# All expert-down units as paired products, with 14 low parts per layer made by an accumulating transfer

## The chip, the cores and the metric

The kernel runs on one core of one Trainium2 chip. The metric is device time in microseconds (us) of that core for one call, and less is better. The engines are TensorE (PE; its weight loads are PEld), VectorE (DVE), ScalarE (ACT), GpSimd (POOL) and SyncE (SP).

## What is computed

A two-layer encoder over 256 tokens of width 1024, all float32. Layer 0 mixes tokens by windowed attention, layer 1 by a gated MLP; after each comes a PEER block, in which every token picks experts among 16384 by product keys:

```python
q = (x @ w_query).reshape(T, PEER_HEADS, 2, D_HALF)
s = jnp.einsum('thcd,hckd->thck', q, sub_keys)
s1, i1 = lax.top_k(s[:, :, 0], PEER_TOPK); s2, i2 = lax.top_k(s[:, :, 1], PEER_TOPK)
...
top_s, pos = lax.top_k(cand, PEER_TOPK)          # 16 of 256 pairs of keys, per token and head
gate = jax.nn.softmax(top_s, axis=-1)
a = jax.nn.gelu(jnp.einsum('cd,chkd->chk', xc, expert_down[ic]))
y = jnp.einsum('chk,chkd->cd', a * gc, expert_up[ic])
```

There are 8 heads with 16 experts each. The kernel gathers no expert weights: it multiplies all 16384 experts with all tokens and lets the gates select.

## The kernel before

**Units.** Weights come in units of 128 x 1024 float32 (512 KB). One layer has its mixer's units, 16 query units, 128 down units (unit n holds experts 128 n to 128 n + 127 of `peer_down`) and 128 up units. Four units are a group; the down phase has groups 0 to 31.

**Two parts per operand.** A float32 product is made of products of rounded parts. For each unit SP loads the raw weights into one of four buffers `raw` (`load`, line 335, or `stream`); ACT rounds them into `w_hi` (`split_hi`, L519) two units ahead; DVE subtracts, `w_lo = raw - w_hi`, in two halves (`split_lo_halves`, L839, and `split_lo_half`, L847). `w_hi` and `w_lo` have four buffers each. The activations stand as `x_both`, high and low part side by side.

**A down unit on PE** has one of two forms. `transposed` (L1491 to L1493) runs 24 matmuls of 256 columns: `w_hi x_hi`, `w_lo x_hi`, `w_hi x_lo` for each of eight slices, and needs `w_lo` at once. `pairs` (L1517, L1521) runs eight matmuls of 512 columns, `w_hi` against high and low part together, then eight of 256 columns, `w_lo x_hi`, and needs `w_lo` only for these. A paired product leaves two sums in one PSUM bank: ACT copies one out (`evict`, L742) and DVE adds the other (`sum_of`, L1314). Which down units are paired is written in the table `PAIRED`: groups 0 to 6 and 21 to 31 wholly, groups 7 to 13 the units 0 and 2 of each four, groups 14 to 20 none. That is 86 of 128.

**DVE beside it.** During the query phase and the first 101 down units DVE also searches the best keys of 16 items (2 token tiles x 8 heads), about one item every seven units; the order of its pieces between the low parts is written out by hand.

**POOL beside it** scatters the gates into a table in HBM (`scatter`, L453): 16 items of 16 indirect transfers with 128 elements each, 256 a layer. Their pace is written in `PACE_FROM`: before each pair of them POOL waits for one more unit to be `used` by PE. Pair p, counted from 0, waits until down unit p - 6 is finished. The transfers of one tile also wait for those of its last head (`added`). The first up units need the finished table: SP loads its pieces into `g_t` (L383 for the first token tile, L386 for the second) once all of that tile's transfers have landed, and DVE multiplies with them (L1411 and L1422).

**Semaphores.** `landed` counts raw loads, `hi_done` and `lo_done` the two parts in order of units, `used` the units that PE has finished. SP waits with a load for the `lo_done` of the unit that had the buffer before.

Of the kernel before, what the change touches and what calls it, by code (L numbers as in the profile page):

```python
# [81 lines left out]

PAIRED = ((0, 7, 4), (7, 14, 2), (14, 21, 0), (21, 32, 4))


def paired(n):

    for first, stop, of_four in PAIRED:
        if first <= n // GROUP < stop:
            return n % GROUP in {0: (), 2: (0, 2), 4: (0, 1, 2, 3)}[of_four]  # L90


# [34 lines left out]
def build(nc, x, attn_units, sg_units, query_units, down_units, up_units, sub_keys, rel_table, bucket_map, sink,  # L127
# [5 lines left out]
    with ExitStack() as ctx:  # L133
# [96 lines left out]

        gain_row = part(HI + 10240, D)

        psum = ctx.enter_context(nc.psum_tensor("psum", [P, 8, 512], F32))
# [13 lines left out]
        hi_done = sem("hi_done")  # L247
        lo_done = sem("lo_done")
        used = sem("used")
        p1_read = sem("p1_read")  # L250
# [78 lines left out]
        l0 = [dict(mix=0, up=MIX_OPERANDS), dict(mix=MIX_OPERANDS + NK, up=MIX_OPERANDS + NK + FT)]  # L329

        block = ctx.enter_context(nc.Block())


        @block.sync
        def _(sp):
            def load(n, source, i=0):

                if not (isinstance(i, int) and n < RAW):
                    sp.wait_ge(lo_done, i * GROUP + (n - RAW + 1))
                sp.dma_start(raw[n % RAW][:, :], source).then_inc(landed[n % RAW], 16)  # L340
# [18 lines left out]
            for layer in range(DEPTH):  # L359
# [8 lines left out]
                stream(u["query"], QUERY_UNITS, queries, 1)  # L368
                stream(u["down"], NK, rows(down_units[layer]))

# [28 lines left out]
        def _(pool):  # L399
# [40 lines left out]
            def scatter(layer):  # L440

                pool.wait_ge(zeroed, 16 * (layer + 1) * (NK // ZERO_UNITS))
                flat = bass.AP(gates[layer].tensor, 0, [[1, NK * P * T], [1, 1]])
                for m in range(ITEMS):
                    t, head = m % TT, m // TT
                    pool.wait_ge(gate_done, ITEMS * layer + m + 1)
                    pool.wait_ge(named, ITEMS * layer + m + 1)
                    if head:
                        pool.wait_ge(added[layer][t], 16 * TOPK * head)
                    for k in range(TOPK):  # L450
                        if k % 2 == 0:
                            pool.wait_ge(used, unit0[layer]["query"] + PACE_FROM[m] + k // 2)
                        pool.indirect_dma_start(flat, bass.IndirectOffsetOnAxis(address[:, TOPK * m + k:TOPK * m + k + 1], 0),  # L453
                                                whole[:, t, head, k:k + 1], None, element_offset=P * t
                                                ).then_inc(added[layer][t], 16)
# [56 lines left out]
        def _(act):  # L512
            def split_hi(n, i=0, group=GROUP):
# [3 lines left out]
                if not (isinstance(i, int) and n < SPLIT):  # L517
                    act.wait_ge(used, i * group + (n - SPLIT + 1))
                act.copy(w_hi[n % SPLIT][:, :], raw[n % RAW][:, :]).then_inc(hi_done, 1)  # L519

# [32 lines left out]
            for layer in range(DEPTH):  # L553
# [184 lines left out]
                def evict(n):  # L738
# [81 lines left out]
        def _(dve):  # L820
# [90 lines left out]
            for layer in range(DEPTH):  # L911
# [404 lines left out]
                def low(n):  # L1316

                    if n and paired(n - 1):
                        sum_of(n - 1)
                    split_lo_halves(u["down"] + n + AHEAD)  # L1320

                def low_first(n):

                    if n and paired(n - 1):
                        sum_of(n - 1)
                    split_lo_half(u["down"] + n + AHEAD, 0)

                def low_second(n):

                    split_lo_half(u["down"] + n + AHEAD, 1)  # L1330

# [156 lines left out]
        def _(pe):  # L1488
            def three(out_ap, hi_s, lo_s, hi_m, lo_m, start, stop):
# [3 lines left out]
                return pe.matmul(out_ap, lo_s, hi_m, start=False, stop=stop)  # L1493

            def transposed(n, bank, read, i=0, group=GROUP, norm=None, amid=None):


                s = n % SPLIT
                pe.wait_ge(lo_done, i * group + (n + 1))
                if read is not None:  # L1500
# [10 lines left out]
            def pairs(n, bank, read, i):  # L1511
# [7 lines left out]
                pe.wait_ge(lo_done, i * GROUP + (n + 1))  # L1519
                for k in range(KD):  # L1520
# [15 lines left out]
            def rows(n, s_l, operands, first, last, i=0, group=GROUP):  # L1536

                pe.wait_ge(lo_done, i * group + (n + 1))
                pe.wait_ge(l_lo_done, operands)
# [28 lines left out]
            for layer in range(DEPTH):  # L1568
# [106 lines left out]
                else:  # L1675
                    def v_columns(i):
                        for c in range(2):
                            for n in range(4):
                                s = (u["mix"] + 4 * c + n) % SPLIT
                                pe.wait_ge(lo_done, i * 8 + (u["mix"] + 4 * c + n + 1))  # L1680
                                for kk in range(2):
# [94 lines left out]
                for c in range(GROUP):  # L1776
                    pe.wait_ge(lo_done, u["up"] + c + 1)
                    pe.wait_ge(l_lo_first, GROUP * layer + c + 1)
# [7 lines left out]
                for c in range(NK - GROUP, NK):  # L1786
                    pe.wait_ge(lo_done, u["up"] + c + 1)
                    pe.wait_ge(l_lo_done, o0 + c + 1)
# [85 lines left out]
```

## Time and profile before

| | |
|---|---|
| Median of 3 runs | 1872.52 us (1872.05 to 1873.03) |
| Span of the profiled execution | 1870.0 us |
| Runs around the span | the median lies 2.5 us above it |
| PE busy | 1844.9 us (99%) |
| DVE, ACT, POOL busy | 78%, 54%, 34% |
| DMA | 420.65 MB, 225 GB/s on average |

The profile is one execution, read from its first to its last instruction. A share of busy time is an average over stages. POOL's time of issuing indirect transfers counts as busy here, that of its direct transfers does not. Where an engine sat idle, a profile line names what ended the wait; "issue" is time in which it waited for nothing that the profile shows. A matmul's duration includes the pipeline, so the distance between two is shorter than one lasts. In layer 0 the down phase runs from about 164 to 526 us, in layer 1 from about 1151 to 1513.

### The profile page before, as it was taken

The numbers are of one execution on the slowest core, as the hardware profiler recorded it, in microseconds if no ns is written. First come the engines' busy times: TensorE is split into PE (matmuls) and PEld (weight loads), VectorE is DVE, ScalarE is ACT, GpSimd is POOL, SyncE is SP. The second block draws the span as 40 slices with busy tenths as digits, with TensorE's granted clock in tenths as the row PEclk, the third lists the DMA queues.
The fourth block names the chain that finished last, engine by engine and source line by source line (L and its number), as shares of the span: only waits on it lengthen the run. The fifth ranks groups of instructions, "written<-read, shape, count | busy, mean of one in ns | idle before, by whom it ended". The sixth has DMA issues, their size and how long they took to land.

```text
span 1870.0 us, 35652 instructions
## 1 busy us (share of the span) xinstructions
PE 1844.9 (99%) x10528; PEld 1613.3 (86%) x10528; DVE 1464.1 (78%) x3510; ACT 1005.2 (54%) x1678; POOL 633.0 (34%) x626
## 2 busy tenths in 40 slices
PE   7999999999999999999999999999999999999998
PEld 6878899998888888888899988899998888888887
DVE  5879999998677766667577789999998676667676
ACT  5655554455465565555444455554455455655554
POOL 1405777778710000000102104777777710000000
PEclk9999999999999999999999999999999999999999
DMA  7985666666678778986859845666666678777775
GB/s 232 344 296 172 190 189 183 186 180 198 192 244 242 241 242 281 289 304 198 303 163 327 287 164 163 192 192 182 184 185 190 193 231 248 240 241 241 242 242 186
DMA packets 159646, 420.65 MB, mean 225 GB/s; under 512 B 32443, under 2 KB 66267, under 8 KB 159036
## 3 DMA queue, kind: packets, MB, share of 16 engines
q1 hardware_dynamic: 130844, 371.32, 64.4%
q0 software_dynamic: 28704, 48.07, 7.6%
q8 instruction: 55, 0.90, 0.2%
q14 instruction: 43, 0.35, 0.1%
HBM read 382.30 MB, written 37.00 MB: 224 GB/s over the span
## 4 chain that ended last, share of the span: by engine, by line
PE 94%; DVE 3%; DMA 2%; ACT 1%; issue 1%; SPq 0%; POOL 0%; DVEq 0%; POOLq 0%; ACTq 0%
PE psum L1491 21%; PE psum L1493 21%; PE psum L1492 21%; PE psum L1517 19%; PE psum L1521 10%; PE psum L1739 1%; DVE w_lo L831 1%; DMA raw<-in_query 1%; PE psum L1706 1%; DMA g_t<-gates 1%; DVE big L905 0%; DMA raw<-in_attn_units 0%; PE psum L1607 0%; PE psum L1596 0%; PE psum L1628 0%
## 5 line engine op out<-in xcount | busy, mean ns | idle before, releaser
L519 ACT CAST w_hi<-raw 128x1024 fp32r<-128x1024 f32 x636 | 669.1, 1053 | 308.5 <-PE psum L1493 284.1
L453 POOL DMA_INDIRECT gates<-whole,address x512 | 558.3, 1090 | 251.3 <-issue 157.1
L1491 PE MATMUL psum<-w_hi,l_hi 128*128 128x512 f32 x1152 | 452.6, 393 | 1.7 <-DVE l_lo L1416 0.7
L1493 PE MATMUL psum<-w_hi,l_lo 128*128 128x512 f32 x1152 | 449.1, 390 | 0.0
L1492 PE MATMUL psum<-w_lo,l_hi 128*128 128x512 f32 x1152 | 448.8, 390 | 0.0
L831 DVE TENSOR_TENSOR w_lo<-raw,w_hi 128x1024 fp32r<-128x1024 f32 x348 | 421.9, 1219 | 30.9 <-ACT w_hi L519 30.9
L1517 PE MATMUL psum<-x_both,w_hi 128*128 128x512 f32 x1616 | 407.5, 394 | 0.0
L1517 PEld LDWEIGHTS psum<-x_both,w_hi 128*128 128x128 f32 x1616 | 290.5, 189 | 51.9
L742 ACT COPY big<-psum 128x256 f32<-128x256 f32 x256 | 95.3, 372 | 352.3 <-PE psum L1521 229.8
L847 DVE TENSOR_TENSOR w_lo<-raw,w_hi 128x512 fp32r<-128x512 f32 x392 | 266.7, 684 | 22.2 <-ACT w_hi L519 19.3
L1491 PE MATMUL psum<-x_both,w_hi 128*128 128x256 f32 x960 | 274.7, 286 | 6.4 <-DVE x_both L893 4.5
L1493 PE MATMUL psum<-x_both,w_lo 128*128 128x256 f32 x960 | 272.6, 284 | 0.0
L1492 PE MATMUL psum<-x_both,w_hi 128*128 128x256 f32 x960 | 272.6, 284 | 0.0
L1491 PEld LDWEIGHTS psum<-w_hi,l_hi 128*128 128x128 f32 x1152 | 216.4, 188 | 48.1 <-issue 2.0
L1493 PEld LDWEIGHTS psum<-w_hi,l_lo 128*128 128x128 f32 x1152 | 216.3, 188 | 45.5
L1405 DVE TENSOR_TENSOR l_lo<-big,l_hi 128x256 fp32r<-128x256 f32 x248 | 105.5, 425 | 191.1 <-ACT l_hi L760 190.9
L1492 PEld LDWEIGHTS psum<-w_lo,l_hi 128*128 128x128 f32 x1152 | 216.5, 188 | 43.1
L1521 PEld LDWEIGHTS psum<-x_both,w_lo 128*128 128x128 f32 x1616 | 220.5, 191 | 15.8
L1521 PE MATMUL psum<-x_both,w_lo 128*128 128x256 f32 x1616 | 225.3, 283 | 0.0
L1491 PEld LDWEIGHTS psum<-x_both,w_hi 128*128 128x128 f32 x960 | 184.7, 192 | 10.8 <-DVE w_lo L831 5.0
L1492 PEld LDWEIGHTS psum<-x_both,w_hi 128*128 128x128 f32 x960 | 184.9, 193 | 0.9
L1493 PEld LDWEIGHTS psum<-x_both,w_lo 128*128 128x128 f32 x960 | 184.9, 193 | 0.0
(156 smaller groups left out, 1591.2 us busy)
## 6 DMA issues: line engine op xcount, KB each, us to landing
raw<-in_down SPq DMA_DIRECT2D x256, 512.0 KB
raw<-in_up SPq DMA_DIRECT2D x256, 512.0 KB
raw<-in_sg_units SPq DMA_DIRECT2D x72, 512.0 KB
gates<-zeros POOLq DMA_DIRECT2D x64, 512.0 KB, 7.1
g_t<-gates SPq DMA_DIRECT2D x248, 128.0 KB, 4.3
raw<-in_query SPq DMA_DIRECT2D x32, 512.0 KB
raw<-in_attn_units SPq DMA_DIRECT2D x20, 512.0 KB
gates<-whole,address POOLq DMA_INDIRECT x512
```

Of the source, the lines that this page charges most:

```text
L453: pool.indirect_dma_start(flat, bass.IndirectOffsetOnAxis(address[:, TOPK * m + k:TOPK * m + k + 1], 0), whole[:, t, head, k:k + 1], None, ...
L519: act.copy(w_hi[n % SPLIT][:, :], raw[n % RAW][:, :]).then_inc(hi_done, 1)
L742: act.copy(acts[:, n, :], psum[:, 4 + n % P1_BANKS, half:half + T]).then_inc(p1_read, 1)
L831: dve.tensor_tensor(w_lo[n % SPLIT][:, :], raw[n % RAW][:, :], w_hi[n % SPLIT][:, :].bitcast(F32), ALU.subtract).then_inc(lo_done, 1)
L847: ins = dve.tensor_tensor(w_lo[n % SPLIT][:, c], raw[n % RAW][:, c], w_hi[n % SPLIT][:, c].bitcast(F32), ALU.subtract)
L1405: dve.tensor_tensor(l_lo[n % GROUP][:, :].rearrange("p (o t) -> p o t", o=1), acts[:, bass.ds(i * GROUP + n, 1), :], l_hi[n % GROUP][:, :] ...
L1491: pe.matmul(out_ap, hi_s, hi_m, start=start, stop=False)
L1492: pe.matmul(out_ap, hi_s, lo_m, start=False, stop=False)
L1493: return pe.matmul(out_ap, lo_s, hi_m, start=False, stop=stop)
L1517: pe.matmul(psum[:, 4 + bank, :], w_hi[s][:, k * P:k * P + P], x_both[:, k, :, :].rearrange("p b t -> p (b t)"), start=k == 0, stop=False)
L1521: ins = pe.matmul(p1[bank], w_lo[s][:, k * P:k * P + P], x_hi[:, k, :], start=False, stop=k == KD - 1)
L1706: ins = pe.matmul(pg[j % 2][:, t * P:t * P + P], v_norm[j % 2][:, t, :], wsp[:, bass.ds(i * 2 + j, 1), :].rearrange("p o q -> p (o q)"), s ...
```

## The change

`PAIRED` now pairs all 128 down units of each layer. To make room on DVE, unit 3 of each group 7 to 20 (units 31, 35, ..., 83; 14 a layer) gets its low part in another way. Its raw weights are loaded into one of two buffers of their own, `raw_aside`, cut from a free part of `big`. ACT rounds them into `w_hi` as always and, four units ahead, writes `w_lo = -round(raw)` (`begin_low`), right after it has evicted unit n - 4. POOL then adds the raw weights to `w_lo` by an accumulating transfer from SBUF to SBUF, which stands in its list between the two indirect transfers of a pair. PE waits for `low_moved` before it takes that low part. All counts of `lo_done` leave the moved units out (`lows`), and SP's loop over the down units is written out for groups 7 to 21.

```diff
-PAIRED = ((0, 7, 4), (7, 14, 2), (14, 21, 0), (21, 32, 4))
+PAIRED = ((0, 32, 4),)
...
+MOVED_GROUPS, MOVED_COLUMN = range(7, 21), 3
+def moved(n):
+    return n // GROUP in MOVED_GROUPS and n % GROUP == MOVED_COLUMN
...
+        raw_aside = [part(HI + 8192 + D * s, D) for s in range(2)]
...
+        def lows(unit):
+            return unit + 1 - sum(is_moved(v) for v in range(unit + 1))
+        def moves(unit):
+            return sum(is_moved(v) for v in range(unit + 1))
+        def raw_of(unit):
+            if is_moved(unit):
+                return raw_aside[moves(unit) % 2]
+            return raw[unit % RAW][:, :]
...
             def load(n, source, i=0):
                 if not (isinstance(i, int) and n < RAW):
-                    sp.wait_ge(lo_done, i * GROUP + (n - RAW + 1))
+                    sp.wait_ge(lo_done, i * GROUP + lows(n - RAW))
...
+                for n in range(GROUP * first, GROUP * stop):
+                    unit = u["down"] + n
+                    if moved(n):
+                        sp.wait_ge(hi_done, unit - RAW + 1)
+                        if moved(n - 2 * GROUP):
+                            sp.wait_ge(low_moved, 16 * moves(unit - 2 * GROUP))
+                    else:
+                        sp.wait_ge(lo_done, lows(unit - RAW))
+                    sp.dma_start(raw_of(unit), down_units[layer][n]).then_inc(landed[unit % RAW], 16)
...
                     for k in range(TOPK):
+                        at = unit0[layer]["query"] + PACE_FROM[m] + k // 2
                         if k % 2 == 0:
-                            pool.wait_ge(used, unit0[layer]["query"] + PACE_FROM[m] + k // 2)
+                            pool.wait_ge(used, at)
+                        elif is_moved(at + SPLIT - 1):
+                            unit = at + SPLIT - 1
+                            pool.wait_ge(low_begun, moves(unit))
+                            pool.dma_start(w_lo[unit % SPLIT][:, :].bitcast(F32), raw_of(unit), accum_op=ALU.add
+                                           ).then_inc(low_moved, 16)
                         pool.indirect_dma_start(flat, ...
...
+                def begin_low(unit):
+                    act.wait_ge(landed[unit % RAW], 16 * (unit // RAW + 1))
+                    act.wait_ge(used, unit - SPLIT + 1)
+                    act.activation(w_lo[unit % SPLIT][:, :], raw_of(unit), ACT.Copy, scale=-1.0).then_inc(low_begun, 1)
...
                     evict(n)
+                    if moved(n + SPLIT):
+                        begin_low(u["down"] + n + SPLIT)
...
-                    split_lo_halves(u["down"] + n + AHEAD)
+                    if not moved(n + AHEAD):
+                        split_lo_halves(u["down"] + n + AHEAD)
...
+            def low_ready(n, i=0):
+                if is_moved(n):
+                    pe.wait_ge(hi_done, n + 1)
+                    pe.wait_ge(low_moved, 16 * moves(n))
+                else:
+                    pe.wait_ge(lo_done, i * GROUP + lows(n))
```

`low_first` and `low_second` on DVE leave the moved units out in the same way, and every wait of PE for a low part goes by `low_ready`.

What this does to the order on **POOL**: below is its list at the first moved unit, first before, then with the change. `gates0` is layer 0's table, and L453 (now L513) an indirect transfer.

```order
L453 DMA gates0<-whole,address 4194304x1 [waits added0_0,used,named,gate_done]
L453 DMA gates0<-whole,address 4194304x1
L453 DMA gates0<-whole,address 4194304x1 [waits used]
L453 DMA gates0<-whole,address 4194304x1
L453 DMA gates0<-whole,address 4194304x1 [waits used]
```

```order
L513 DMA gates0<-whole,address 4194304x1 [waits added0_0,used,named,gate_done]
L513 DMA gates0<-whole,address 4194304x1
L513 DMA gates0<-whole,address 4194304x1 [waits used]
L511 DMA w_lo3<-big 128x1024 [waits low_begun]
L513 DMA gates0<-whole,address 4194304x1
L513 DMA gates0<-whole,address 4194304x1 [waits used]
```

The accumulating transfer has come between the two indirect ones of a pair; the other 255 keep their places. The same happens 13 more times a layer, every fourth pair.

On **ACT**, at the first moved units (L742, now L802, is the eviction of a down unit, L519, now L579, the rounding of a unit two further on), before and with the change:

```order
L742 COPY big<-psum 128x256 [waits used]
L519 CAST w_hi<-raw 128x1024 [waits used,landed2]
L742 COPY big<-psum 128x256 [waits used]
L519 CAST w_hi<-raw 128x1024 [waits used,landed3]
L742 COPY big<-psum 128x256 [waits used]
```

```order
L802 COPY big<-psum 128x256 [waits used]
L808 ACTIVATE w_lo<-big 128x1024 [waits used,landed3]
L579 CAST w_hi<-raw 128x1024 [waits used,landed2]
L802 COPY big<-psum 128x256 [waits used]
L579 CAST w_hi<-big 128x1024 [waits used,landed3]
L802 COPY big<-psum 128x256 [waits used]
```

A negated copy stands behind an eviction, and the next rounding comes after it; the moved unit's own rounding reads from `big`, where `raw_aside` lies.

On **PE**, a moved unit (`w_lo` of buffer 3), first before, where its form is cut after two of eight slices, then with the change:

```order
L1491 MATMUL psum<-x_both,w_hi3 128x256 [waits p1_read,lo_done]
L1492 MATMUL psum<-x_both,w_hi3 128x256
L1493 MATMUL psum<-x_both,w_lo3 128x256
...
L1491 MATMUL psum<-x_both,w_hi0 128x256 [waits p1_read,lo_done]
```

```order
L1596 MATMUL psum<-x_both,w_hi 128x512 [waits p1_read,hi_done,summed]
L1596 MATMUL psum<-x_both,w_hi 128x512 x7
L1600 MATMUL psum<-x_both,w_lo 128x256 [waits low_moved,hi_done]
L1600 MATMUL psum<-x_both,w_lo 128x256 x7
L1596 MATMUL psum<-x_both,w_hi 128x512 [waits p1_read,hi_done,summed]
```

The wait for the low part has moved from the unit's first matmul to its ninth, and it is now one for `low_moved`.

## Rows read from the trace of the kernel before

**Rows 1.** The page, busy time of the engines (busy us, share of the span, instructions)

```profile
PE 1844.9 (99%) x10528; PEld 1613.3 (86%) x10528; DVE 1464.1 (78%) x3510; ACT 1005.2 (54%) x1678; POOL 633.0 (34%) x626
```

**Rows 2.** Windows: PE, PEld, DVE, ACT, POOL busy (x); clock; DMA share, GB/s

```profile
242.80:322.30 79.50, 79.50 (x563) 74.83 (x562) 75.52 (x257) 39.88 (x77) 58.29 (x54) 1.00 0.66 185
322.30:402.90 80.60, 80.60 (x673) 80.60 (x672) 75.49 (x243) 39.88 (x76) 62.94 (x58) 1.00 0.66 182
```

**Rows 3.** The chain that ended last, layer 0 (start us, us, what)

```profile
241.87 0.95 PE psum L1521 x8
...
316.57 1.84 PE psum L1517 x8
402.89 1.84 PE psum L1517 x8
```

**Rows 4.** Groups of POOL, 242.8 to 402.9 us (busy us, mean ns | idle before, releasers)

```profile
L453 POOL DMA_INDIRECT gates<-whole,address x112 | 122.6, 1095 | 39.2 <-issue 35.1 <-PE psum L1493 3.4 <-PE psum L1521 0.4
```

**Rows 5.** Timeline of POOL, layers 0 and 1 (start us, us, what [idle before])

```profile
313.45 1.43 POOL L453 DMA_INDIRECT gates<-whole,address  x1 [3.59 <-issue]
...
325.11 0.96 POOL L453 DMA_INDIRECT gates<-whole,address  x1 [0.30 <-issue]
326.38 0.96 POOL L453 DMA_INDIRECT gates<-whole,address  x1 [0.30 <-issue]
...
1300.58 1.04 POOL L453 DMA_INDIRECT gates<-whole,address  x1 [3.21 <-issue]
```

**Rows 6.** Timeline: eviction of unit 82 and first transfer of pair 88, layers 0 and 1

```profile
400.04 0.37 ACT L742 COPY big<-psum 128x256 f32<-128x256 f32 x1 [1.49 <-PE psum L1493]
402.62 1.32 POOL L453 DMA_INDIRECT gates<-whole,address  x1 [0.30 <-DVE whole L1233]
...
1387.56 0.37 ACT L742 COPY big<-psum 128x256 f32<-128x256 f32 x1 [1.56 <-PE psum L1493]
1388.40 1.43 POOL L453 DMA_INDIRECT gates<-whole,address  x1 [0.30 <-issue]
```

**Rows 7.** Groups of DVE, 242.8 to 402.9 us: halves of low parts, and sums

```profile
L847 DVE TENSOR_TENSOR w_lo<-raw,w_hi 128x512 fp32r<-128x512 f32 x112 | 76.8, 685 | 8.5 <-ACT w_hi L519 6.6 <-issue 1.0
L1314 DVE TENSOR_TENSOR big<-psum,big 128x256 f32<-128x256 f32 x15 | 6.2, 415 | 0.1
```

**Rows 8.** Groups of ACT, 242.8 to 402.9 us: roundings, and evictions

```profile
L519 ACT CAST w_hi<-raw 128x1024 fp32r<-128x1024 f32 x56 | 58.8, 1050 | 0.0
L742 ACT COPY big<-psum 128x256 f32<-128x256 f32 x56 | 20.9, 373 | 80.2 <-PE psum L1493 59.6 <-PE psum L1521 20.6
```

**Rows 9.** Timeline of POOL: three transfers back to back, and one behind another

```profile
62.34 2.24 POOL L436 DMA_DIRECT2D gates<-zeros  x3 [1.69 <-PE psum L1493]
...
823.94 0.53 POOL L430 DMA_DIRECT2D big<-in_sub_keys  x1
```

**Rows 10.** Landings of POOL's 512 KB transfers: L436 (zeros), then L505 (h_kept)

```profile
DMA to landing us min/median/max: 3.7/7.1/19.1
...
DMA to landing us min/median/max: 6.4/7.4/7.5
```

**Rows 11.** The start of the up phases: second halves of the gates, and the page's issues

```profile
524.68 2.12 SPq L386 DMA_DIRECT2D g_t<-gates  x4
529.90 0.89 DVE L1422 TENSOR_TENSOR big<-big,g_t 128x128 f32<-128x128 f32 x4
...
1509.91 1.85 SPq L386 DMA_DIRECT2D g_t<-gates  x4
1518.18 0.89 DVE L1422 TENSOR_TENSOR big<-big,g_t 128x128 f32<-128x128 f32 x4
...
g_t<-gates SPq DMA_DIRECT2D x16, 64.0 KB, 3.2
```

**Rows 12.** DMA queues, 322.3 to 402.9 us (packets, MB, share of 16 engines)

```profile
q1 hardware_dynamic: 3998, 14.54, 63.3%
```

More of the change, by code:

```diff
@@ L90, in paired, with moved_until @@
             return n % GROUP in {0: (), 2: (0, 2), 4: (0, 1, 2, 3)}[of_four]
+MOVED_GROUPS, MOVED_COLUMN = range(7, 21), 3
+def moved(n):
+    return n // GROUP in MOVED_GROUPS and n % GROUP == MOVED_COLUMN
+def moved_until(n):
+    return sum(moved(m) for m in range(n))
 def paired_until(n):
@@ L248, in build @@
         lo_done = sem("lo_done")
+        low_begun = sem("low_begun")
+        low_moved = sem("low_moved")
         used = sem("used")
@@ L329, in build, with is_moved @@
         l0 = [dict(mix=0, up=MIX_OPERANDS), dict(mix=MIX_OPERANDS + NK, up=MIX_OPERANDS + NK + FT)]
+        down_of = {e["down"] + n: (layer, n) for layer, e in enumerate(unit0) for n in range(NK)}
+        def is_moved(unit):
+            return unit in down_of and moved(down_of[unit][1])
+        def lows(unit):
[6 more added lines that the diff above has]
+            return raw[unit % RAW][:, :]
         block = ctx.enter_context(nc.Block())
@@ L368, in _ @@
                 stream(u["query"], QUERY_UNITS, queries, 1)
-                stream(u["down"], NK, rows(down_units[layer]))
+                downs = rows(down_units[layer])
+                first, stop = MOVED_GROUPS.start, MOVED_GROUPS.stop + 1
+                with sp.Fori(0, first) as i:
+                    for c in range(GROUP):
+                        load(u["down"] + c, downs(i, c), i)
+                for n in range(GROUP * first, GROUP * stop):
[7 more added lines that the diff above has]
+                    sp.dma_start(raw_of(unit), down_units[layer][n]).then_inc(landed[unit % RAW], 16)
+                with sp.Fori(stop, NK // GROUP) as i:
+                    for c in range(GROUP):
+                        n = u["down"] + c
+                        sp.wait_ge(lo_done, i * GROUP + (lows(n + GROUP * (stop - 1)) - GROUP * stop))
+                        sp.dma_start(raw[n % RAW][:, :], downs(i, c)).then_inc(landed[n % RAW], 16)
                 def up_weights(c, i):
@@ L518, in split_hi @@
                     act.wait_ge(used, i * group + (n - SPLIT + 1))
-                act.copy(w_hi[n % SPLIT][:, :], raw[n % RAW][:, :]).then_inc(hi_done, 1)
+                act.copy(w_hi[n % SPLIT][:, :], raw_of(n)).then_inc(hi_done, 1)
             def squares_first(z):
@@ L1325, in low_first @@
                         sum_of(n - 1)
-                    split_lo_half(u["down"] + n + AHEAD, 0)
+                    if not moved(n + AHEAD):
+                        split_lo_half(u["down"] + n + AHEAD, 0)
                 def low_second(n):
-                    split_lo_half(u["down"] + n + AHEAD, 1)
+                    if not moved(n + AHEAD):
+                        split_lo_half(u["down"] + n + AHEAD, 1)
                 low(0)
@@ L1493, in three @@
                 return pe.matmul(out_ap, lo_s, hi_m, start=False, stop=stop)
+            def low_ready(n, i=0):
[4 more added lines that the diff above has]
+                    pe.wait_ge(lo_done, i * GROUP + lows(n))
             def transposed(n, bank, read, i=0, group=GROUP, norm=None, amid=None):
                 s = n % SPLIT
-                pe.wait_ge(lo_done, i * group + (n + 1))
+                low_ready(n, i)
                 if read is not None:
@@ L1518, in pairs @@
                               start=k == 0, stop=False)
-                pe.wait_ge(lo_done, i * GROUP + (n + 1))
+                low_ready(n, i)
                 for k in range(KD):
@@ L1536, in rows @@
             def rows(n, s_l, operands, first, last, i=0, group=GROUP):
-                pe.wait_ge(lo_done, i * group + (n + 1))
+                low_ready(n, i)
                 pe.wait_ge(l_lo_done, operands)
@@ L1679, in v_columns @@
                                 s = (u["mix"] + 4 * c + n) % SPLIT
-                                pe.wait_ge(lo_done, i * 8 + (u["mix"] + 4 * c + n + 1))
+                                pe.wait_ge(lo_done, i * 8 + lows(u["mix"] + 4 * c + n))
                                 for kk in range(2):
@@ L1776, in _ @@
                 for c in range(GROUP):
-                    pe.wait_ge(lo_done, u["up"] + c + 1)
+                    low_ready(u["up"] + c)
                     pe.wait_ge(l_lo_first, GROUP * layer + c + 1)
@@ L1786, in _ @@
                 for c in range(NK - GROUP, NK):
-                    pe.wait_ge(lo_done, u["up"] + c + 1)
+                    low_ready(u["up"] + c)
                     pe.wait_ge(l_lo_done, o0 + c + 1)
```

## The prediction

> **What bounds the kernel now.** I read the page first: TensorE (PE) is busy 99% of the span [rows 1], so whatever else changes matters only where it makes PE wait or takes matmul time away. Next, the windows by stage: the two stretches are units 28 to 55 and 56 to 83 of the first layer's down phase; PE is busy for the whole of each at full granted clock, VectorE (DVE) for 94% or more [rows 2]. Then the chain of work that ended last, for the price of one unit: a paired unit is 1.84 us of eight 512-column matmuls and 0.95 us of eight 256-column ones, 2.79 us together. The piece at 316.57 begins unit 54, which is paired, the one at 402.89 begins unit 84, and the 29 units between them are not; so one of these takes (402.89 - 316.57 - 2.79) / 29 = 2.88 us [rows 3].
>
> Last I looked at GpSimd (POOL), which does no arithmetic here but issues two indirect transfers per unit. Over the same 160.1 us it issued 112 of them, 1095 ns each, and of its 39.2 us of idle time 35.1 us ended in nothing the profile shows [rows 4]: 0.30 us between any two, and one hole of 3.59 us [rows 5]. So 112 x 0.30 + 3.3 = 36.9 us are its own time, and only 2.3 us were real waiting for its pace. POOL is all but full, and it is late: count the pairs from the scatter's start. Pair 88 may go when unit 82 has finished; unit 82's eviction starts at 400.04, the pair at 402.62, 2.6 us late. In layer 1 the same two are 1387.56 and 1388.40, 0.8 us late [rows 6].
>
> **PE's part.** 14 units of groups 7 to 13 and 28 of groups 14 to 20 become paired: 42 x (2.88 - 2.79) = 42 x 0.087 = 3.65 us a layer, 7.3 us in all. That is the whole possible gain.
>
> **DVE's part.** Per layer 42 sums (415 ns) are added and 14 low parts (two halves of 685 ns) leave [rows 7]: 17.4 - 19.2 = -1.8 us. It is uneven: groups 7 to 13 lose 9.6 and gain 5.8 us; groups 14 to 20 lose 9.6 and gain 11.6 us, so 75.5 us [rows 2] become 77.5 in 28 x 2.79 = 78.2 us. That fits, with PE's own lead of 1.84 us (a paired unit needs its low part only after its first eight matmuls) as new cover. Cost: nothing; it is a rival below.
>
> **ACT's part.** 14 negated copies a layer, priced like its 1050 ns casts, beside 80.2 us of waiting in 160 [rows 8]: nothing. Each stands right behind an eviction and delays the next cast by about a microsecond once in four units, which DVE's missing low part covers. **SP's part.** The moved weights land in buffers of their own; SP waits for the cast (hi_done) and for the accumulation two groups earlier, both long past, and the same number of loads is issued. The loads are issued in order, so a moved unit's load cannot pass its neighbour's. Nothing.
>
> **POOL's part, the term that decides.** Each moved low part puts one more transfer into POOL's full list, between the two indirects of a pair. The accumulating issue is not in the trace. The nearest rows: direct transfers of 128 rows stand 0.53 us apart, those cut in 512 pieces 2.24 / 3 = 0.75 us [rows 9]; a whole indirect with its gap is 0.96 + 0.30 = 1.26 us [rows 5]. I take 0.75, since an addition must name its bytes more than once, and keep 0.53 and 1.26 as bounds. 14 x 0.75 = 10.5 us a layer; 2.3 us fall into the waiting that POOL has. POOL is then dP = 8.2 us later than before at the last moved unit (bounds 5.1 and 15.3).
>
> Who waits for it: PE, for the low part of unit 83. POOL may issue it once unit 79 is finished, say at U, but comes L late, first issues one indirect (1.26), then the transfer lands T later, and PE needs another 0.95 us of matmuls. Before, unit 83 ended at U + 4 x 2.88 = U + 11.5. The delay is L + dP + 1.26 + T + 0.95 - 11.5 = L + dP + T - 9.3. For T the nearest rows are POOL's 512 KB transfers: median 7.1 us for the zeroing ones with a fastest of 3.7, 6.4 to 7.5 for h_kept's [rows 10]. I take 7.1; bounds 3.7 and 10.7 (below). Layer 0: 2.6 + 8.2 + 7.1 - 9.3 = 8.6 us. Layer 1: 0.8 + 8.2 + 7.1 - 9.3 = 6.8 us. The pairing gain is already inside, since the comparison is with unpaired units.
>
> The second place where POOL's lateness is paid: the up phase needs the finished gates. SP issues the second half at 524.68 once the scatter is complete, such a piece takes 3.2 us, and DVE uses it at 529.90: 2.0 us of slack; in layer 1 from 1509.91 to 1518.18, 5.1 us [rows 11]. That gives 8.2 - 2.0 = 6.2 and 8.2 - 5.1 = 3.1 us. It is the same lateness, not another, so the larger of the two counts.
>
> **Sum.** 8.6 + 6.8 = 15.4 us on a span of 1870.0. The median of the runs is 1872.5, 2.5 us above that span, which I leave: 1870.0 + 15.4 + 2.5 = 1887.9, so **1888 us**.
>
> A rule against the size of this term: the Trainium skill (SBUF — State Buffer, "Who interferes with whom") says that a tensor_tensor with both inputs in SBUF holds a port pair against GpSimd operations that read SBUF; a low part is one, a sum with its PSUM input is not. The trace is compatible: indirects take 0.96 us at their shortest and 1095 ns on average, 15 us more over 112. If a quarter of the low parts, 14 of 57, took their share of that along, POOL would get back up to 3.7 us a layer, and the sum would be 1880.5.
>
> **The rivals.**
> *The transfer is the slow part (T).* The accumulation reads both buffers and writes one. The load queue is busy 63.3% of 80.6 us for 28 loads, 1.82 us each over all 16 engines [rows 12]; one more pass, contending with as much of loads, is T = 7.1 + 2 x 1.8 = 10.7. Then no lateness is needed: from unit n - 4's end, 0.3 + 1.26 + 10.7 = 12.2 us against the 3 x 2.79 + 1.84 = 10.2 that PE gives it, 2.0 us short, 14 times a layer: 28 - 3.65 = 24 us, 49 in all, 1921 us. It decides from T = 8.6 on. For it: a second read; against: a source in SBUF needs no HBM. Chance 0.15. The Trainium skill (Collectives: The Full Stack, "The bandwidth ceiling: the fold count and why AG ≠ RS ≠ AR") has the add emit two read descriptors per chunk and run at about half a copy's rate; no run so far shows it.
>
> *Issue and transfer are both cheap.* 0.53 us and T = 3.7: dP = 5.1; layer 0 then pays at the gates, 5.1 - 2.0 = 3.1 us, layer 1 0.8 + 5.1 + 3.7 - 9.3 = 0.3 us, 1876 us. Chance 0.17, of which 0.07 within 0.2%.
>
> *The other side: POOL absorbs the issues.* The place is the 3.6 us hole in each layer's scatter and the 0.30 us between indirects [rows 5]. If the added issues fall into these, so that dP is 0 or below, and T is under some 5 us, layer 0 gains up to 3.65 and layer 1 3.65 us: 1865 us. It decides from dP below about 2 us. Against it: indirects stand back to back with exactly this 0.30 between them, so it belongs to each issue. Chance 0.09.
>
> *DVE becomes the bound* in units 56 to 83. With 77.5 of 78.2 us it needs only some 1 us more of waiting for ACT's later casts per seven units: four such stretches a layer, 8 us less the gain of 7.3, about 1873 us. For it: 94% busy, and 5.1 us of idle time in that stretch become 0.7 [rows 2]; against: a late low part has the new cover of 1.84 us. Chance 0.04. *The change does not do what it says*, PE takes the low part from somewhere in time anyway and the pair costs what it did: 1872.5. PE's list shows the wait, so 0.03.
>
> **How the numbers follow.** A measurement of this kernel can tell about 0.2%, 3.7 us, from no change. The forecast's own case (1880 to 1902, the upper end from an issue of 1.26 us: 15.7 + 13.9 = 29.6 us) has 0.52. Slower by over 0.2%: 0.52 + 0.15 + 0.10 of the cheap case + 0.03 of DVE's = 0.80. Within: 0.07 + 0.04 + 0.01 = 0.12. Faster: 0.08. The range runs from 1874, inside the cheap case, to 1908, inside the slow-transfer case.
>
> **What would show it.** In the new profile: the accumulating issues at 0.5 to 0.9 us on POOL; POOL's pairs falling further behind from group 7 on, by about 0.4 us per group; the first PE waits for the moved low part near the 3.6 us hole, about unit 50, and growing stalls to unit 83; units of 2.79 us between them; no PE wait for DVE. I am wrong if PE never waits for low_moved, if stalls begin at the very first moved unit (then T is over 8.6), or if PE waits for w_lo from DVE.

## The result, and the profile after

The changed kernel takes **1891.8 us** (median of 4 runs, 1890.9 to 1895.0) against 1872.3 us for the kernel before beside it: a ratio of 1.0104, 95% interval 1.0092 to 1.0116, so 19.5 us slower. Forecast were 1888 us and a range of 1874 to 1908. The forecast's sign, size and place were right. How the time is lost was right in half of its steps only, and that the sum comes so near is in part luck.

In the changed kernel's numbering L1596 and L1600 are the paired matmuls (512 and 256 columns), L511 is the accumulating transfer, L513 the indirect one, L802 ScalarE's eviction, L808 its negated copy, L915 a half of a low part and L1382 the sum of a pair. First the page of the changed kernel (busy time, software queue, chain), then TensorE's waits (us in total, times, longest).

```profile
span 1889.9 us, 34054 instructions
PE 1847.5 (98%) x9856; PEld 1583.1 (84%) x9856; DVE 1461.2 (77%) x3538; ACT 1031.2 (55%) x1706; POOL 655.8 (35%) x654
...
q0 software_dynamic: 32736, 62.75, 12.1%
...
PE 85%; DMA 4%; DVE 4%; POOL 3%; issue 2%; ACT 1%; SPq 0%; DVEq 0%; POOLq 0%; ACTq 0%
```

```profile
PE psum L1600 <- DMA w_lo<-big: 14.5, 7, 3.8
PE psum L1562 <- DVE x_both L961: 4.2, 4, 2.8
```

TensorE was never idle for a transfer in a down phase before [rows 2]; now it waits 14.5 us for a moved low part, in seven places. The windows of units 28 to 83, both layers, and GpSimd's groups in the first of them, show how much and who is busy:

```profile
243.30:410.60 167.30, 160.49 (x898) 139.85 (x897) 147.76 (x509) 93.19 (x167) 132.34 (x126) 0.98 0.81 218
1239.20:1406.20 167.00, 159.26 (x897) 138.38 (x897) 150.82 (x523) 93.41 (x168) 131.57 (x128) 0.99 0.82 221
```

```profile
L513 POOL DMA_INDIRECT gates<-whole,address x112 | 119.2, 1065 | 34.8 <-issue 32.2 <-PE psum L1600 2.6
L511 POOL DMA_DIRECT2D w_lo<-big x14 | 13.7, 980 | 0.5 <-ACT w_lo L808 0.4
```

These units took 160.1 us in layer 0 [rows 2], and as long in layer 1; they take 167.3 and 167.0, together 14.1 us more. The accumulating issue costs 0.98 us, and GpSimd has 0.5 + 2.6 us of waiting left in 167. (POOL's busy time in these windows holds both kinds of issue, 112 indirect and 14 direct ones, and not the indirect ones alone.)

One of the seven stalls, from the chain that ended last (start us, us, what), and the windows after four of them (PE, PEld, DVE, ACT, POOL busy, granted clock, DMA share, GB/s):

```profile
276.93 1.84 PE psum L1596 x8
278.77 0.97 PE psum L1600 x8
279.74 0.03 issue
279.77 1.02 POOL gates L513
280.79 8.40 DMA w_lo<-big
289.18 0.14 issue
289.32 1.81 PE psum L1600 x8
291.13 2.77 PE psum L1596 x8
```

```profile
289.30:293.00 3.70, 3.68 (x13) 3.28 (x14) 0.42 (x1) 1.83 (x3) 2.50 (x4) 0.54 0.73 248
385.20:389.00 3.80, 3.39 (x13) 3.15 (x14) 2.29 (x6) 1.30 (x3) 2.89 (x4) 0.56 0.76 230
1285.00:1289.00 4.00, 4.00 (x18) 3.33 (x18) 1.15 (x3) 2.26 (x3) 3.15 (x4) 0.66 0.69 205
1404.70:1408.50 3.80, 3.80 (x15) 3.22 (x16) 3.49 (x20) 1.32 (x2) 3.02 (x3) 0.64 0.64 188
```

The low parts of the other six stalls but one are in the chain too, those of units 71 and 75 of layer 0 and of units 43, 63 and 83 of layer 1 (start and time to landing):

```profile
364.69 6.98 DMA w_lo<-big
376.86 8.61 DMA w_lo<-big
1276.44 8.18 DMA w_lo<-big
1336.41 8.08 DMA w_lo<-big
1395.86 8.67 DMA w_lo<-big
```

**Five of the seven stalls, 12.3 of the 14.5 us, belong to transfers that took 8.1 to 8.7 us.** In these five the first packet moves 3.7 to 5.0 us after the issue; in the other 23 it moves after 1.5 to 2.2 us, and only two of them, units 67 and 71 of layer 0, stall TensorE at all (1.5 and 0.8 us). So a stall here is lateness of GpSimd and, mostly, a late start of the transfer together.

The timeline has the eviction of unit 39, whose end releases this pair of GpSimd's, and the pair's first indirect:

```profile
276.97 0.38 ACT L802 COPY big<-psum 128x256 f32<-128x256 f32 x1 [1.65 <-PE psum L1600]
279.77 1.03 POOL L513 DMA_INDIRECT gates<-whole,address  x1 [0.30 <-PE psum L1600]
```

GpSimd is 2.8 us late (the releaser named in the second row is only the last event before it; the pair before ended at 279.46); the accumulation is issued at 280.79 and lands 8.4 us later. TensorE had finished unit 43's wide matmuls at 287.2 and stood for 2.2 us. What then follows was in no step of the forecast: the eight 256-column matmuls take 1.81 us and the next eight wide ones 2.77, where 0.95 and 1.84 are usual [rows 3]. The granted clock of that stretch is near its lower level (0.54, 1.2 GHz being 0.50). That is 4.58 - 2.79 = 1.8 us on top of the wait, and 1.6 to 1.8 us at four of the seven stalls; the kernel before had 1.00 throughout here [rows 2].

So for units 28 to 83: waits 14.5, lower clock 6.9 in four stretches (some 1.7 each), less the pairing's gain 2 x 3.65 = 7.3, makes 14.1 us, which is what the windows show. The remaining 5.8 us of the 19.9 between the two spans: 2 us in the rest of the down phases, nearly all of it in units 84 to 99, 3.1 us at the very end of the program (below), under 1 us elsewhere.

### The profile page after: what moved, and what is told of

Its sections match the earlier page's. It is cut to its first block, busy times and chain, and to the rows that moved or that the text cites. A ratio compares the mean times of both kernels' runs of the same rounds, so it can differ in the third digit from the quotient of the medians.

```text
span 1889.9 us, 34054 instructions
## 1 busy us (share of the span) xinstructions
PE 1847.5 (98%) x9856; PEld 1583.1 (84%) x9856; DVE 1461.2 (77%) x3538; ACT 1031.2 (55%) x1706; POOL 655.8 (35%) x654
## 3 DMA queue, kind: packets, MB, share of 16 engines
q0 software_dynamic: 32736, 62.75, 12.1%
## 4 chain that ended last, share of the span: by engine, by line
PE 85%; DMA 4%; DVE 4%; POOL 3%; issue 2%; ACT 1%; SPq 0%; DVEq 0%; POOLq 0%; ACTq 0%
PE psum L1596 22%; PE psum L1562 16%; PE psum L1564 16%; PE psum L1563 16%; PE psum L1600 12%; POOL gates L513 3%; DMA w_lo<-big 3%; PE psum L1818 1%; DMA g_t<-gates 1%; DVE w_lo L899 1%; DMA raw<-in_query 1%; PE psum L1785 1%; DVE big L973 0%; DMA raw<-in_attn_units 0%; DVE w_lo L915 0%
## 5 line engine op out<-in xcount | busy, mean ns | idle before, releaser
L579 ACT CAST w_hi<-raw 128x1024 fp32r<-128x1024 f32 x608 | 639.0, 1052 | 310.5 <-PE psum L1564 283.7
L513 POOL DMA_INDIRECT gates<-whole,address x512 | 553.5, 1081 | 235.1 <-issue 142.5
L1596 PE MATMUL psum<-x_both,w_hi 128*128 128x512 f32 x2288 | 580.0, 396 | 0.0
L1596 PEld LDWEIGHTS psum<-x_both,w_hi 128*128 128x128 f32 x2288 | 414.0, 190 | 74.7
L1600 PEld LDWEIGHTS psum<-x_both,w_lo 128*128 128x128 f32 x2288 | 313.1, 192 | 41.1 <-issue 17.3
L1600 PE MATMUL psum<-x_both,w_lo 128*128 128x256 f32 x2288 | 321.9, 284 | 14.8 <-DMA w_lo<-big 14.5
L802 ACT COPY big<-psum 128x256 f32<-128x256 f32 x256 | 96.0, 375 | 335.0 <-PE psum L1600 334.5
L915 DVE TENSOR_TENSOR w_lo<-raw,w_hi 128x512 fp32r<-128x512 f32 x336 | 228.7, 685 | 33.2 <-ACT w_hi L579 32.8
L907 DVE TENSOR_TENSOR w_lo<-raw,w_hi 128x512 fp32r<-128x512 f32 x184 | 118.9, 687 | 43.7 <-ACT w_hi L579 43.5
L1382 DVE TENSOR_TENSOR big<-psum,big 128x256 f32<-128x256 f32 x256 | 106.7, 417 | 34.7 <-ACT big L802 33.4
L1471 DVE TENSOR_TENSOR big<-big,g_t 128x256 f32 (+1 forms) x248 | 103.9, 419 | 6.6 <-DMA g_t<-gates 6.5
L490 POOL DMA_DIRECT2D gates<-zeros x64 | 48.4, 760 | 162.3 <-PE psum L1564 136.4
L828 ACT CAST l_hi<-big 128x256 fp32r (+1 forms) x248 | 98.5, 398 | 0.0
```

The lines of the kernel that those rows point to most:

```text
L579: act.copy(w_hi[n % SPLIT][:, :], raw_of(n)).then_inc(hi_done, 1)
L907: ins = dve.tensor_tensor(w_lo[n % SPLIT][:, c], raw[n % RAW][:, c], w_hi[n % SPLIT][:, c].bitcast(F32), ALU.subtract)
L915: ins = dve.tensor_tensor(w_lo[n % SPLIT][:, c], raw[n % RAW][:, c], w_hi[n % SPLIT][:, c].bitcast(F32), ALU.subtract)
L1382: dve.tensor_tensor(acts[:, n, :], p1[n % P1_BANKS], acts[:, n, :], ALU.add).then_inc(summed, 1)
L1600: ins = pe.matmul(p1[bank], w_lo[s][:, k * P:k * P + P], x_hi[:, k, :], start=False, stop=k == KD - 1)
```

## The experiments

Two groups of chips have to be kept apart. On one (the comparison above, and chip 3) the kernel before takes 1872 us; on the other (chips 8, 10 and 13) it takes 1923 to 1925. **Each run is compared by its ratio to the kernel before on the same chip**, and where runs of two chips are set side by side, the text says so. The profile of the kernel before on chip 10 says where these 50 us lie:

*b_again*: no edit.

> The kernel before, for its profile on this chip: where its 50 us more lie. If ScalarE's late evictions are a matter of the chip, they are there too, in the down phase of both layers (some 25 us in each, evictions up to 5 us after TensorE has finished a unit), with full groups of 2.8 us elsewhere; if they come with the changed program, this trace looks like the first one and only the totals differ.

```profile
ACT w_hi L519 <- PE psum L1493: 289.2, 252, 2.2
ACT big L742 <- remote: 195.0, 73, 7.6
ACT big L742 <- PE psum L1521: 144.6, 82, 4.8
```

1924.6 us (one run). The first expectation holds: outside the down phases it keeps the pace of the fast chip within some 2 us, the down phases take some 25 us longer each, and ScalarE's evictions wait for a release that the profile gives to nobody ("remote", none on the fast chip). I found no cause. TensorE has waits there that the fast chip has not. That a stall of the changed kernel can fall into one of them, and so cost less, is my reading and not shown.

**Is it GpSimd's lateness?** The decisive pair ran on a chip of the fast group (chip 3). *a_third* is the change unedited; *e9_fewer_indirects* leaves out the indirect transfer behind each accumulation:

```
+    if left_out(layer, m, k):
+        continue
     pool.indirect_dma_start(flat, ...).then_inc(added[layer][t], 16)
```

`left_out` is true for the second indirect of a pair that carries a moved low part; the counts awaited on `added` are lowered to match.

> The changed kernel without the indirect transfer behind each moved low part: 28 of 512 indirects are left out, so 28 columns of the gates stay zero. GpSimd gives up 14 x 1.26 = 17.6 us a layer and pays 14 x 0.98 = 13.7 us for the accumulations, so it is never later than before. If the lateness is the cause, TensorE waits for a moved low part hardly at all (under 2 us in all; even the slow landings of 8.4 us fit: 0.3 + 1.26 + 8.4 = 10.0 of 10.2 us), and the time is that of the change without its waits: about 0.008 below the change in ratio on a chip where that costs 1.010, about 0.002 to 0.003 below it where it costs 0.999. If the transfer is slow by itself or its queue stands still whatever GpSimd's lateness, half or more of the stalls stay, and the ratio is within 0.002 of the change's.

> The changed kernel once more, beside the run with fewer indirects on the same chip: ratio 1.010 if the chip runs the kernel before in 1872 us, 0.997 to 1.001 if in 1923.

a_third: 1892.5 us, ratio 1.0111 (1.0096 to 1.0127): the result repeats. e9: 1873.2 us, ratio 1.0002 (0.9993 to 1.0011). Below, of a_third and then of e9, who waited for the accumulation and its landing; then e9's waits of TensorE for low parts and its windows of units 28 to 55 and 56 to 83.

```profile
L511 POOL DMA_DIRECT2D w_lo<-big x28: 940/980/997, 246.3 to 1397.9; - x28
...
who waited for it (us, times):
  PE psum L1600: 12.3, 8
...
DMA to landing us min/median/max: 4.6/5.7/8.9
```

```profile
L519 POOL DMA_DIRECT2D w_lo<-big x28: 940/972/995, 244.6 to 1377.1; - x28
...
DMA to landing us min/median/max: 4.6/5.8/7.9
```

```profile
PE psum L1610 <- DVE w_lo L925: 2.1, 2, 1.2
```

```profile
245.70:323.90 78.20, 78.20 (x449) 68.82 (x448) 71.95 (x258) 46.50 (x84) 57.84 (x56) 1.00 0.86 233
323.90:402.10 78.20, 78.20 (x449) 68.70 (x449) 73.88 (x244) 45.72 (x83) 60.31 (x55) 1.00 0.83 230
```

The transfers are the same in number and issue time and nearly so in landing (at most 7.9 us, against 8.9), and nobody waits for them. Units 28 to 83 take 2 x 78.2 = 156.4 us where they took 160.1: the pairing's full 3.65 us, and full clock. So without the lateness the transfers cost nothing. The late starts remain, two in place of four in a_third (3.8 and 3.6 us, unit 67 of each layer): GpSimd's pair is only 0.24 us late there, and the low part has landed 9.6 and 8.8 us after the eviction of four units before, where TensorE gives 10.2. In a_third the same kind of transfer meets a lateness of 2.4 to 3.7 us and stalls TensorE for 1.7 to 4.0 us, 10.6 of the 12.3 us in all. The run takes the lateness away and two late starts with it, so how the gain divides between these two stays open. The expected 0.008 below the change came out as 0.0109. That e9 still doesn't beat the kernel before lies in two places: the stretch behind the moved units takes 47.0 us where it took 44.7 (and 45.9 in layer 1), with VectorE at 46.17 us of work in it (before 44.28), and the program's end is 3.4 us longer. In that stretch TensorE has one wait for VectorE's low part, 1.2 us; how the rest of the 2.3 us comes about isn't shown.

```profile
402.10:449.10 47.00, 45.67 (x258) 38.88 (x257) 46.17 (x123) 22.44 (x43) 36.51 (x33) 1.00 0.64 186
```

```profile
402.90:447.60 44.70, 44.70 (x257) 39.36 (x257) 44.28 (x119) 22.83 (x42) 35.86 (x30) 1.00 0.64 189
```

(the first row is e9's, the second that of the kernel before, both units 84 to 99 of layer 0.)

**What the addition costs against a copy** (chip 13). *e3_copy*:

```
-    pool.dma_start(w_lo[...].bitcast(F32), raw_of(unit), accum_op=ALU.add)
+    pool.dma_start(w_lo[...].bitcast(F32), raw_of(unit))
```

> The changed kernel with a plain copy in the place of the accumulation: the low part of a moved unit becomes its raw weights, so the subtraction of the rounded part is left out. Issues, waits and the bytes written stay. If the rate of the adding transfer matters, the copy's packets take about half of the adding ones' 327 ns and it lands some 1.3 us sooner: each of the seven long stalls shrinks by about 1.3 us and the two or three shortest go, with their half-clock stretches: 10 to 14 us less, ratio to before 1.003 to 1.005. If only GpSimd's lateness and the stand-stills of its queue count, the stalls stay what they are: ratio 1.009 to 1.011. If the adding is the whole trouble, the ratio is 0.996.

1915.8 us, ratio 0.9956 (0.9941 to 0.9972). The change itself, on chip 10 with the same time before:

*a_again*: no edit.

> The changed kernel itself beside the experiments, on their chip, since everything there takes some 50 us longer and only ratios carry over. If the change costs the same there, its ratio to before is 1.009 to 1.012, as at first, and the run with the accumulation ahead of the pair (1.0033) is the better order by some 12 us. If the slower chip hides the moved low parts' lateness behind its own late evictions, the ratio is 1.002 to 1.006, and the order of the two issues matters little.

1922.0 us, ratio 0.9988 (0.9974 to 1.0001), below both expectations. The copy is 0.003 faster (two chips side by side), about half of what was expected. Of e3, its issue, TensorE's waits for it and the queue's row on the page:

```profile
L511 POOL DMA_DIRECT2D w_lo<-big x28: 570/570/575, 250.1 to 1416.4; - x28
...
  PE psum L1600: 9.3, 4
```

```profile
q0 software_dynamic: 32736, 62.75, 9.5%
```

The copy is issued in 0.57 us, the addition in 0.98. On the DMA engines the 28 moved parts (62.75 - 48.07 = 14.7 MB, 3584 packets of 4 KB) raise the queue's share from 7.6 to 12.1% as additions: 0.121 x 16 x 1889.9 - 0.076 x 16 x 1870.0 = 1385 us, 0.39 us a packet; and to 9.5% of e3's span of 1913.9 us as copies (7.4% of 1915.2 in e6 below, which has none): some 640 us, 0.18 us. An addition runs at about half a copy's rate, as the Trainium skill has it (Collectives: The Full Stack, "The bandwidth ceiling: the fold count and why AG ≠ RS ≠ AR"). But the eight packets per engine are some 3 us of a landing of 5.7; halving them leaves four stalls. The copy also takes 0.4 us less of GpSimd's time at each of the 28 issues, which the expectation left out, so the 0.003 isn't the packets' rate alone.

**Who needs the accumulation at all** (chip 8). *e2_no_add* drops the transfer and lets TensorE wait for the negated copy alone; *e5_add_elsewhere* issues it, into a scratch tensor in HBM that nobody reads (not shown: each addition also waits until the one before has landed, four units earlier):

```
-    pool.dma_start(w_lo[...].bitcast(F32), raw_of(unit), accum_op=ALU.add).then_inc(low_moved, 16)
+    pool.dma_start(aside_sum[moves(unit) - 1], raw_of(unit), accum_op=ALU.add).then_inc(low_moved, 16)
-    pe.wait_ge(low_moved, 16 * moves(n))
+    pe.wait_ge(low_begun, moves(n))
```

> Leaves out the accumulating transfers: w_lo of the 28 moved units stays minus the rounded weights, and PE waits for ACT's negated copy alone. All else is as in the change: pairing, ACT's 28 copies, SP's buffers. Theory A: the whole loss goes and the full gain of the pairing comes, 1865 us (1864 to 1867). Rival B (ACT's late casts or DVE's sums are what PE waits for): stays above 1872.

> The accumulating transfers are issued at the same places with the same source and size, but add into a scratch tensor in HBM, and PE waits for ACT's negated copy alone (the moved low parts are minus the rounded weights). POOL bears the full price of issuing (14 times 0.98 us and a gap), PE no longer waits. It separates the lateness at the gates from the wait for the low part. Theory A: the late scatter is paid only at the start of the up phases, 2 to 6 us in layer 0 and little in layer 1: 1867 to 1873 us. Rival D (the additions hurt by their load on the DMA engines, loads of raw weights come late): 1880 or more, with ACT waiting for raw<-in_down.

Ratios 0.9965 (0.9950 to 0.9980) and 0.9971 (0.9958 to 0.9985). Without the wait for the landing e2 takes 5.7 us less than before by the medians, most of the pairing's 7.3 us. With the same 28 issues on GpSimd (984 ns each) and as many bytes, though written to HBM, e5 is as fast as e2: on this chip GpSimd's lateness has no second place where it is paid. The later gates and the load on the DMA engines cost nothing that these runs can tell. Together with e9: the issues without the wait cost nothing here, and there the wait without the lateness costs nothing.

**A better place for the issue?** *e4_add_first* (chip 8) puts the accumulation ahead of the pair's first indirect:

```
-    elif is_moved(at + SPLIT - 1):
+    if k % 2 == 0 and is_moved(at + SPLIT - 1):
```

> The accumulating transfer stands ahead of the pair's first indirect transfer instead of between the two, nothing else. Theory A (a moved low part lands at lateness + 1.26 + T after unit n - 4's end, and PE can wait until 10.2): 1.26 us less on that chain shortens each of the 7 stalls of 2 to 4 us and ends some, with the half clock that follows them: 1878 to 1885 us. Rival C (the transfer's own time, over 8.4 us wherever it stalls, decides; its place in the list does not): 1889 or more, since POOL may wait for ACT's copy first.

1930.4 us, ratio 1.0033 (1.0016 to 1.0050); it was to gain, and is 8 us slower than a_again (another chip, but with the same time before). What GpSimd waited for before its issues:

```profile
L511 POOL DMA_DIRECT2D w_lo<-big x28: 938/966/995, 247.9 to 1427.5; - x28
its engine sat idle before it (us, times) until:
  ACT w_lo L808: 10.3, 5
```

The negated copy begins only behind ScalarE's eviction, and the wait for it now holds up both indirects of the pair too. In the change's order the first indirect covers most of it (0.4 us in the group above, 3.0 us in a_again). In the down phases TensorE waits less for the transfers (13.4 us against 17.7 in a_again, as `--source L511` counts them) and more for everything else (26.3 us against 16.6), most of it in waits that the profile gives to nobody. So the expected shortening of the stalls is there in part and is outweighed; that GpSimd's longer waiting does this isn't shown, and the two runs are on different chips.

**VectorE as the bound.** *e1_pair_only* (chip 8) and *e6_pair_again* (chip 13) pair everything and move nothing; *e7_pair_part* (chip 10) also leaves groups 14 to 20 half paired (the last two lines, its alone):

```
-MOVED_GROUPS, MOVED_COLUMN = range(7, 21), 3
+MOVED_GROUPS, MOVED_COLUMN = range(7, 7), 3
-PAIRED = ((0, 32, 4),)
+PAIRED = ((0, 14, 4), (14, 21, 2), (21, 32, 4))
```

> All 128 down units paired, no low part moved. Theory A (lateness of POOL and the landing of the addition cause all of the loss): PE never waits for an addition here, but DVE gets 42 sums more and no low part less: 75.5 + 5.8 = 81.3 us of work in 78.2 us for units 28 to 55, 75.5 + 11.6 = 87.1 in 78.2 for units 56 to 83, so some 12 us over less 3.65 us a layer: 1885 to 1889 us, with PE waits for w_lo from DVE. Rival (DVE has hidden slack and needed no relief): 1865 us.

> The pairing of all groups without any moved low part, once more, because on the chip of the first look everything was some 50 us slower and ScalarE's evictions came late, so that the price of a full VectorE could not be read. If VectorE is the bound of such a kernel (per layer 28 sums of 415 ns more in groups 14 to 20, 14 more in groups 7 to 13, nothing taken away: 17.4 us more work, of which some 5 us fall into idle time), it takes 8 to 17 us more than before: 1881 to 1889, ratio 1.004 to 1.009, with waits of TensorE for VectorE's low part. If VectorE has room, the pairing's gain of 7.3 us shows: 1865, ratio 0.996.

> No low part moved; groups 0 to 13 and 21 to 31 paired in all four units, groups 14 to 20 in two of four: 28 units more per layer in products of 512 columns than before, where VectorE still has room by the windows (groups 14 to 20: 75.5 plus 5.8 us in 78.2 to 80). Gain 28 x 0.087 = 2.4 us a layer, 4.9 us in all, ratio 0.997, if VectorE keeps up; if its 94% busy share was already the limit, what it adds (5.8 us per stretch and layer) comes back as TensorE waits, up to 15 us, ratio 1.001 to 1.008.

Ratios 0.9986 (0.9971 to 1.0000), 0.9967 (0.9954 to 0.9980) and 0.9996 (0.9982 to 1.0009). TensorE does wait for VectorE's low parts here (e6):

```profile
PE psum L1600 <- DVE w_lo L915: 6.5, 13, 1.2
```

but the feared 8 to 17 us did not come on these chips. Since TensorE there has other waits under which VectorE catches up, they don't say what the pairing alone costs where the kernel before takes 1872 us. That stays open, and so does why e7 gains less than e6.

**Half as many moved parts.** *e8_every_other* (chip 10):

```
-    return n // GROUP in MOVED_GROUPS and n % GROUP == MOVED_COLUMN
+    return n // GROUP in MOVED_GROUPS and n // GROUP % 2 == 0 and n % GROUP == MOVED_COLUMN
```

> Every second moved low part only (groups 8, 10 to 20: 7 a layer), all groups paired. GpSimd then gets 7 x 0.98 = 6.9 us a layer in place of 13.7, most of which its 2.3 us of waiting and the 3.6 us hole hold. If each transfer costs by its own delay, the transfer stalls are half of the change's; if they come from the lateness that adds up, nearly all go and TensorE waits for GpSimd's transfers under 3 us in all. VectorE has 75.5 + 11.6 - 5.5 = 81.6 us of work in 78.2 us of groups 14 to 20 and may cost up to 3.4 us a layer. Ratio to before between 0.997 and 1.002 by the lateness theory, 1.003 to 1.006 if each transfer costs by itself.

1916.0 us, ratio 0.9957 (0.9942 to 0.9972): 6 us faster than the change and 8.8 us faster than the kernel before, both on the same chip, so it beats both there. (SP's wait before it reuses a buffer of `raw_aside` is fitted to the smaller count, not shown.) TensorE's wait for the transfers falls from 13.1 to 8.7 us (17.7 to 12.0 with the one stall in each that the list of waits gives to nobody). That is neither the half that a price per transfer would give nor under 3 us, as a lateness that only adds up would have it, so on this chip neither account is enough. On a chip of the fast group it wasn't run.

## Why the prediction was right, step by step

- **PE's gain, 0.087 us per unit.** Right: e9's units 28 to 83 are 3.7 us shorter per layer.
- **The accumulating issue, taken as 0.75 us** between 0.53 and 1.26. Undersized: 0.98 us. The copy's 0.57 shows that the addition is what makes it longer.
- **T, the landing, taken as 7.1 us** between 3.7 and 10.7. Mis-sized, and not one number: median 5.7 (a_third), but 8.1 to 8.7 us in five of the seven that stall, those with the late starts. At 8.1 to 8.7 us and the 10.2 us that TensorE gives, less than some 1 us of lateness is enough for a stall, by an estimate with about 1 us for the indirect between; at 5.7 us it takes over 3 us. With 5.7 and 0.98 the forecast's formula gives 2.6 + 11.4 + 5.7 - 9.3 = 10.4 and 8.6 us.
- **GpSimd falls behind until unit 83, and the delay is paid there.** This step failed. The lateness grows by about 0.6 us a group (predicted 0.4), but a stall of TensorE gives GpSimd the time back: after the one at unit 43 the next pair is 0.24 us behind its release again. So the loss comes in seven separate stalls, the first at unit 43 and not at 50. That the sum of seven stalls comes close to that of one growing delay is luck as far as the runs show: most of it hangs on the late starts, which the forecast didn't have.
- **No term for the clock.** Missing: 6.9 us. In the sum it is made up for by terms that were too large: the holes of 3.6 us [rows 5] are gone, and the indirects take 1065 ns in place of 1095 [rows 4], so of layer 0's 13.7 us of issues GpSimd is charged 165.1 - 157.7 = 7.4 (busy and issue time of its groups, after less before), where the forecast has 8.2 beyond its waiting. The sum of 15.4 us stands against 16.0 measured in the down phases, with errors in it that cancel.
- **The rule on shared ports** (1880.5 us). The indirects did get shorter, by 3.4 us a layer where up to 3.7 was allowed. But e1, where every low part stays on VectorE, has 1079 ns over all 512 and the change 1081 (before 1090), on another chip. So what the Trainium skill says there (SBUF — State Buffer, "Who interferes with whom") isn't needed for most of it, and no run tests it alone.
- **The gates as a second place to pay.** Right to count only the larger: nothing is paid there in the changed kernel (under 1 us outside the down phases and the end), nor in e5 on its chip.
- **The rivals.** A transfer slow by itself (49 us) is refuted by e9 and by the median of 5.7 us; but its condition, T from 8.6 us on, is nearly met or met by five of the 28, and that is where most of the stalls are. Both cheap: the issue is not, and T is 4.6 us at best. GpSimd absorbs the issues: only in e9, where it was given the time; the 3.6 us hole did vanish, which that rival wanted, and this was not enough. VectorE as the bound: 1.2 us in the changed kernel's repeat, 2.1 in e9; small, where it was put.

## What to carry to other kernels

A transfer whose consumer has a fixed deadline must be costed as lateness of the issuing engine plus landing, not by either, and the landing by its slow cases (8 to 9 us here) and not by its median (5.7); if the engine is full, take work off its list before adding to it, which here was worth 19 us for 14 indirects a layer. Price each stall of TensorE of about 2 us higher than it is, since a stretch at the lower clock can follow. And on an engine that works its list in order, an issue with a wait in front holds up what stands behind it: moving the addition ahead of its pair raised GpSimd's wait before it from 3.0 to 10.3 us and made nothing faster.

## What the runs showed of the hardware

- The four stalls of 2.0 to 3.8 us were followed by a stretch at the lower clock level and 1.6 to 1.8 us lost on top; the three shorter ones, up to 1.9 us, were not. In a_third the three of 2.3 to 4.0 us were, the five up to 1.7 us were not.
- The program's end is longer wherever the additional transfers are issued by GpSimd, added or copied, 14 or 28 of them: from VectorE's last piece of the chain to the end of the span 6.0 us in the changed kernel (1883.86 to 1889.9) against 2.9 us before (1867.13 to 1870.0). From the last matmul it is 10.2 to 10.5 us (counted from its start) in the eight traces with them, 6.9 to 8.1 us in the six without. The place is GpSimd's closing DRAIN, the wait for its own engine that ends its list: it takes 7.8 to 7.9 us in the eight traces and 3.5 us in the six. In the changed kernel SyncE has seen the outputs land at 1886.0 and all wait for this DRAIN until 1889.7; before, it was over ahead of the outputs. What it waits for is open. The last pieces of the two chains:

```profile
1883.20 0.66 DVEq L146
```

```profile
1866.47 0.66 DVEq L133
```

- The holes of some 3.6 us in GpSimd's list [rows 5] are in none of the eight traces with the additional transfers. All eight have late starts among these transfers instead: the first packet moves 3.1 to 5.3 us after the issue, in place of the usual 1.1 to 1.5. That these are the same thing in another place is a guess.
- The same programs take 50 us longer on some chips, nearly all of it in the down phases, and a change's sign can differ with it: 1.0104 and 1.0111 on the fast ones, 0.9988 on chip 10.
